# Modulation rows, first norm and five input panels by quarters instead of halves, at the start of a two-block kernel

## What is computed

```python
c_act = jax.nn.silu(c)
mod = c_act @ w_ada[l] + b_ada[l]                 # 2048 -> 6 * 2048
sh1, sc1, g1, sh2, sc2, g2 = [m[:, None, :] for m in jnp.split(mod, N_MOD, axis=-1)]
h = rms_norm(x, norm_mix_g[l]) * (1.0 + sc1) + sh1
proj = h @ w_in[l]                                # 2048 -> 8192
u, q, k, v, ga, gb = jnp.split(proj, split_at, axis=-1)
y_ssm = s5_branch(u, ...)                         # scan over tokens, 64 groups of 64 states
y_att = moba_attention(q, k, v, rel_bias)
merged = sigmoid(ga) * (y_ssm @ w_proj_ssm) + sigmoid(gb) * (y_att @ w_proj_attn)
x = x + g1 * (merged @ w_out[l])
```

## Time and profile before

| | us |
|---|---|
| runs: median (range) | 3000.81 (3000.13 to 3002.28) |
| profiled execution, its own time | 3000.71 |
| its span | 2999.4 |
| busy PE, DVE, ACT, POOL in the span | 2931.9, 2023.6, 1379.4, 239.4 |
| chain that ended last | PE 86%, DVE 7%, DMA 3%, issue 2% |

### The profile page before, as it was taken

The page is one execution under the profiler, slowest core; times in us unless marked ns, Lnnn a source line. Parts: engine busy times, 40 slices in busy tenths (PEclk is TensorE's granted clock), DMA queues, the critical chain, the costliest instruction groups (busy, mean ns, idle before and its releaser), DMA issues.

```text
span 2999.4 us, 42350 instructions
## 1 busy us (share of the span) xinstructions
PE 2931.9 (98%) x17149; PEld 2513.0 (84%) x17149; DVE 2023.6 (67%) x2359; ACT 1379.4 (46%) x1686; POOL 239.4 (8%) x256
## 2 busy tenths in 40 slices
PE   6999999999999999999999999999999999999998
PEld 3778899788888888888989987778898888888886
DVE  5489878997767655556887776674557545555555
ACT  3343344444444444345565655554445444444443
POOL 6835410000000000000000000000000000000000
PEclk9999999999999999999999999999999999999999
DMA  9967688896777766665556565456555666666664
GB/s 350 329 213 210 209 295 297 302 319 203 236 257 257 235 187 193 194 186 172 174 171 196 174 192 155 155 161 195 186 176 175 190 189 188 192 190 192 192 191 149
DMA packets 303520, 631.67 MB, mean 211 GB/s; under 512 B 21872, under 2 KB 26384, under 8 KB 302752
## 3 DMA queue, kind: packets, MB, share of 16 engines
q1 hardware_dynamic: 298496, 618.74, 64.9%
q10 hardware_dynamic: 2800, 5.33, 0.5%
q0 software_dynamic: 2032, 4.90, 0.5%
HBM read 624.68 MB, written 4.21 MB: 210 GB/s over the span
## 4 chain that ended last, share of the span: by engine, by line
PE 86%; DVE 7%; DMA 3%; issue 2%; ACT 1%; ACTq 0%; DVEq 0%
PE PS L1026 16%; PE PS L1042 15%; PE PS L1044 15%; PE PS L1043 15%; PE PS L1030 8%; PE PS L1013 5%; PE PS L1015 5%; PE PS L1014 5%; DVE wlo L1991 2%; DMA raw<-in_w_ada 1%; DVE aacc L1980 1%; ACT whi L2519 1%; PE PS L691 1%; DMA raw<-in_w_in 1%; PE PS L824 1%
## 5 line engine op out<-in xcount | busy, mean ns | idle before, releaser
L1991 DVE TENSOR_TENSOR wlo<-raw,whi 128x1024 fp32r<-128x1024 f32 x857 | 1070.4, 1254 | 729.6 <-ACT whi L2519 729.1
L2519 ACT ACTIVATE whi<-raw 128x1024 fp32r<-128x1024 f32 x857 | 904.5, 1059 | 1077.2 <-PE PS L1044 570.1
L1042 PE MATMUL PS<-whi,R 128*128 128x512 f32 x2144 | 847.2, 395 | 7.3 <-DVE R L1496 5.4
L1043 PE MATMUL PS<-whi,R 128*128 128x512 f32 x2144 | 836.0, 390 | 0.0
L1044 PE MATMUL PS<-wlo,R 128*128 128x512 f32 x2144 | 835.9, 390 | 0.0
L1026 PE MATMUL PS<-R,whi 128*128 128x512 f32 x2048 | 516.5, 394 | 10.8 <-DVE R L1903 5.4
L1042 PEld LDWEIGHTS PS<-whi,R 128*128 128x128 f32 x2144 | 403.0, 188 | 102.1 <-issue 7.6
L1044 PEld LDWEIGHTS PS<-wlo,R 128*128 128x128 f32 x2144 | 402.9, 188 | 85.6
L1043 PEld LDWEIGHTS PS<-whi,R 128*128 128x128 f32 x2144 | 403.2, 188 | 81.5 <-issue 1.0
L1013 PE MATMUL PS<-R,whi 128*128 128x256 f32 x1536 | 439.8, 286 | 7.5 <-DVE wlo L1991 6.0
L1026 PEld LDWEIGHTS PS<-R,whi 128*128 128x128 f32 x2048 | 371.3, 190 | 78.4 <-issue 11.5
(11 more groups left out here) (424 smaller groups left out, 1728.8 us busy)
## 6 DMA issues: line engine op xcount, KB each, us to landing
raw<-in_w_in SPq DMA_DIRECT2D x275, 512.0 KB, 4.3
raw<-in_w_ff SPq DMA_DIRECT2D x175, 512.0 KB, 4.4
raw<-in_w_ada SPq DMA_DIRECT2D x136, 512.0 KB, 5.2
raw<-in_w_mlp_up SPq DMA_DIRECT2D x128, 512.0 KB, 3.8
raw<-in_w_mlp_down SPq DMA_DIRECT2D x128, 512.0 KB, 4.4
...
```

Source lines behind the costliest of these rows:

```text
L1042: pe.matmul(o, hi, whi[:, s, w], start=first, stop=False)
L1043: pe.matmul(o, lo, whi[:, s, w], start=False, stop=False)
L1991: v.tensor_tensor(wlo[:, i % SPN, :], words(j), whi[:, i % SPN, :].bitcast(F32), ALU.subtract).then_inc(lo_done, 1)
L2519: a.activation(whi[:, i % SPN, :], words(j), ACT.Copy).then_inc(hi_done, 1)
```

## The change

- The row units hold 512 columns of sc1's and the same 512 of sh1's part. 16 of them give a quarter: four tiles of h. The row is copied, closed and normed four times, after row units 15, 31, 47 and 63, each time in the tick's own `side`, and ScalarE's copy stands ahead of that tick's weight splitting.
- 27 weight ticks instead of 17 lie between the row ticks, the first after row unit 18 (before: 33), and 30 units are prepared there.
- The five part panels are computed by quarters: 15 panels of two units. ScalarE copies the first quarter's, VectorE adds the second's and third's (`part_more`, 10 new instructions of 128 by 1024); the last quarter is what `both_halves` adds.
- x's transposes, its deviation and the first norm's factor come sooner (ticks 3, 7, 10 instead of 6, 13, 28 after the start), the factor is copied to SBUF; the four matrices' ticks lie between 28 and 62; the branch's input matrix is loaded by ScalarE at row tick 13 instead of at the start.
- x is saved to DRAM in four pieces instead of one. SSM0 is 32 instead of 24. v0 comes ahead of q0 and k0, two of the gb panels are read out one tick later, and the eight attention heads start 5 to 14 and 2 to 11 ticks after k0 and k1 instead of 2 to 11 after v0 and v1.

```diff
-NTAKEN = 17
+QUARTER = 16
+NTAKEN = 27
 NEARLY = NTAKEN + 3
-TAKEN = {33: 0} | {36 + n * 27 // (NTAKEN - 1): n + 1 for n in range(NTAKEN - 1)}
-EARLY = {31: (0,)} | {a - 3: (n,) for a, n in TAKEN.items() if n} | {61 + n: (NTAKEN + n,) for n in range(3)}
+TAKEN = {18 + n * 45 // 26: n for n in range(NTAKEN)}
+EARLY = {a - 3: (n,) for a, n in TAKEN.items()} | {61 + n: (NTAKEN + n,) for n in range(3)}
 NWIDE = 56
 NXN = 16
-SSM0 = 24
+SSM0 = 32
...
-    for i in range(5):
-        panel("part", i, w_in, 0, 8, i * 512 if i < 2 else 4096 + (i - 2) * 512, h, by_h, a_once.at("part%d" % i), i > 1)
+    by_h = lambda k: (h_ready, k + 1)
+    by_quarter = lambda q: lambda k: (h_ready, 4 * q + k + 1)
+    halved = [i * 512 if i < 2 else 4096 + (i - 2) * 512 for i in range(5)]
+
+    for q in range(3):
+        for i, c0 in enumerate(halved):
+            panel("part", 5 * q + i, w_in, 4 * q, 4, c0, h_from[q], by_quarter(q),
+                  (part_added, 5 * q + i - 4) if q else a_once.at("part%d" % i), i > 1)
     for i in range(2):
-        panel("u", i, w_in, 8, 8, i * 512, h_b, by_h_b, (evac_v["u"], i + 1))
+        panel("u", i, w_in, 12, 4, halved[i], h_from[3], by_quarter(3), (evac_v["u"], i + 1))
     for i in range(3):
-        panel("ga", i, w_in, 8, 8, 4096 + i * 512, h_b, by_h_b, v_once.at("ga%d" % i), True)
+        panel("ga", i, w_in, 12, 4, halved[2 + i], h_from[3], by_quarter(3), v_once.at("ga%d" % i), True)
     panel("ga", 3, w_in, 0, 16, 4096 + 1536, h, by_h, (evac_a["ga"], 4), True)
     for i in range(4):
         panel("gb", i, w_in, 0, 16, 6144 + i * 512, h, by_h, (evac_a["gb"], i + 1), True)
     for i in range(2):
-        for name, c0 in (("q", 1024), ("k", 2048), ("v", 3072)):
+        for name, c0 in (("q", 1024), ("k", 2048), ("v", 3072)) if i else (("v", 3072), ("q", 1024), ("k", 2048)):
...
+    def row_src(q, kt):
+        return wada[kt * P:(kt + 1) * P, 0:2 * D].rearrange("p (g d) -> p g d", g=2)[:, :, 512 * q:512 * q + 512]
+
     def weight_unit(n):
         return "w", n, 4 if panel_of[n].nk == 4 else 2, unit_src[n]
 
     for a in range(NADA):
-        units.append(("row", a, 1, ada_src(a % 2, a // 32, a % 32 // 2)))
+        units.append(("row", a, 2, row_src(a // QUARTER, a % QUARTER)))
...
-    row_bank, row_close_bank = (0, 7), (2, 5)
-    rstd1 = PS[:, 4, T:2 * T]
+    row_bank, row_close_bank = (0, 7, 4, 7), 6
+    rstd1 = rstd[:, :]
 
     def norm_tile(k):
-        return PS[:, ((2, 3, 5) if k < 8 else (5, 6, 7))[k % 8 % 3], 0:T]
+        return PS[:, 5 + k % 2, 0:T]
...
-    X_TURN, COLUMNS, STD1, FACTOR1 = -NADA + 6, -NADA + 10, -NADA + 13, -NADA + 28
-    B_TURN, MATRICES_C = -NADA + 11, len(TAKEN) + 2
-    MATRIX = (-NADA + 17, -NADA + 18, -NADA + 19, -NADA + 37)
-    MATRIX_TURN = (-NADA + 23, -NADA + 26, -NADA + 30, -NADA + 40)
-    ROW_CLOSE, NORM1 = [-33, len(TAKEN)], [-32, len(TAKEN) + 1]
+    X_TURN, STD1, COLUMNS, FACTOR1, BIAS, B_TURN = (-NADA + t for t in (3, 7, 8, 10, 11, 22))
+    B_LOAD, X_SAVE = -NADA + 13, [NTAKEN + t for t in (-1, 2, 5, 8)]
+    ANGLES, PARAMETERS, MATRICES_C = -NADA + 17, -NADA + 18, len(TAKEN) + 2
+    MATRIX = (-NADA + 28, -NADA + 40, -NADA + 47, -NADA + 57)
+    MATRIX_TURN = (-NADA + 34, -NADA + 45, -NADA + 53, -NADA + 62)
+    ROW_COPY = [-NADA + 15 + QUARTER * q for q in range(4)]
+    ROW_CLOSE = [-NADA + 15, -NADA + 32, -NADA + 48, len(TAKEN) - 1]
...
-            free[4] = h_ready, 8
+            free[4] = a_once.at("factor1")
 
         def row_matmuls(n, j):
-            q, g, kt = n // 32, n % 2, n % 32 // 2
+            q, kt = n // QUARTER, n % QUARTER
             pe.wait_ge(*landed(j))
             if n == 0:
                 pe.wait_ge(*v_once.at("cact"))
-            if n == 32:
-                wait_bank(row_bank[1])
+            elif kt == 0:
+                wait_bank(row_bank[q])
+                free[row_bank[q]] = row_copied, q + 1
             for part in range(4):
                 o = 32 * part
-                t = pe.matmul(PS[o:o + 1, row_bank[q], g * T:g * T + T], cact[:, kt:kt + 1], words(j)[:, part * T:part * T + T],
-                              start=(n % 32 == 0), stop=(kt == 15), skip_group_check=True)
+                t = pe.matmul(PS[o:o + 1, row_bank[q], 0:T], cact[:, kt:kt + 1], words(j)[:, part * T:part * T + T],
+                              start=(kt == 0), stop=(kt == QUARTER - 1), skip_group_check=True)
             t.then_inc(row_done, 1)
 
         def row_close(q):
-            bank = row_close_bank[q]
             pe.wait_ge(row_copied, q + 1)
-            if q:
-                wait_bank(bank)
-            for g in range(2):
-                for c in range(2):
-                    o = 512 * q + T * g + P * c
-                    t = pe.matmul(PS[:, bank, 8 * g + 4 * c:8 * g + 4 * c + 4], aacc[:, o:o + P], ident[:, 0:P:32],
-                                  start=(g + c == 0), stop=True, skip_group_check=True)
+            wait_bank(row_close_bank)
+            for c in range(2):
+                o = T * q + P * c
+                t = pe.matmul(PS[:, row_close_bank, 4 * c:4 * c + 4], aacc[:, o:o + P], ident[:, 0:P:32],
+                              start=(c == 0), stop=True, skip_group_check=True)
             t.then_inc(row_turned, 1)
-            if q:
-
-                for bank in (4, 5, 6, 7):
-                    free[bank] = (h_ready, 16)
-            yield
+            free[5] = free[6] = h_ready, 4 * q + 4
...
-            s8 = slice(8 * q, 8 * q + 8)
+            s4 = slice(4 * q, 4 * q + 4)
             tile = norm_tile
             v.wait_ge(modrow, q + 1)
-            if q == 0:
-                v.wait_ge(m_copied, 6)
-            v.scalar_tensor_tensor(A1[:, s8], mod[:, 16 + 8 * q:24 + 8 * q], 1.0, cols[:, C_G1 + 8 * q:C_G1 + 8 * q + 8],
+            if turned_in(q):
+                v.wait_ge(m_copied, turned_in(q))
+            v.scalar_tensor_tensor(A1[:, s4], mod[:, 16 + 4 * q:20 + 4 * q], 1.0, cols[:, C_G1 + 4 * q:C_G1 + 4 * q + 4],
                                    ALU.add, ALU.mult).then_inc(v_own, 1)
             v.wait_ge(v_own, vt.one())
-            v.wait_ge(*p_once.at("stat1"))
-            v.wait_ge(*a_once.at("b"))
-            for n in range(10):
+            v.wait_ge(*a_once.at("factor1"))
+            for n in range(6):
                 if n > 1:
-                    k = 8 * q + n - 2
+                    k = 4 * q + n - 2
                     v.wait_ge(n1_hi, k + 1)
                     v.scalar_tensor_tensor(h.lo(k), tile(k), mod[:, k:k + 1], h.hi(k).bitcast(F32),
                                            ALU.add, ALU.subtract).then_inc(h_ready, 1)
-                if n < 8:
-                    k = 8 * q + n
-                    if n > 2:
-                        v.wait_ge(h_ready, k - 2)
+                if n < 4:
+                    k = 4 * q + n
+                    if n > 1:
+                        v.wait_ge(h_ready, k - 1)
                     v.scalar_tensor_tensor(tile(k), X3[:, k, :], A1[:, k:k + 1], rstd1, ALU.mult, ALU.mult).then_inc(n1_scaled, 1)
-                if n == 9:
-                    yield
...
+        def part_more(x):
+            i, q = x.i % 5, x.i // 5
+            v.wait_ge(*passed("part", x.i))
+            v.wait_ge(*(a_once.at("part%d" % i) if q == 1 else (part_added, i + 1)))
+            v.tensor_tensor(half_sum(i), banks(x), half_sum(i), ALU.add).then_inc(part_added, 1)
+            yield
+
         def both_halves(x):
             i = x.i
             v.wait_ge(*passed(x.name, i))
             if x.name == "u":
-                v.wait_ge(*a_once.at("part%d" % i))
+                v.wait_ge(part_added, 6 + i)
                 v.tensor_tensor(fv(U + 1024 * i, 1024), banks(x), half_sum(i), ALU.add).then_inc(evac_v["u"], 1)
             else:
                 if i == 0:
                     v.wait_ge(h_ready, 16)
-                    v.wait_ge(x_saved, 16)
-                v.wait_ge(*a_once.at("part%d" % (2 + i)))
+                v.wait_ge(x_saved[i], 16)
+                v.wait_ge(part_added, 8 + i)
...
+        def x_save(p):
             a.wait_ge(x_copied, 8)
-            a.dma_start(scr_x, fv(XT, 4096)).then_inc(x_saved, 16)
+            a.dma_start(scr_x[:, 1024 * p:1024 * p + 1024], fv(XT + 1024 * p, 1024)).then_inc(x_saved[p], 16)
...
-            a.wait_ge(row_done, 32 * q + 32)
-            a.copy(aacc[:, 512 * q:512 * q + 512], PS[:, row_bank[q], :]).then_inc(row_copied, 1)
+            a.wait_ge(row_done, QUARTER * (q + 1))
+            a.copy(aacc[:, T * q:T * q + T], PS[:, row_bank[q], 0:T]).then_inc(row_copied, 1)
...
+            if n in ROW_COPY:
+                row_copy(ROW_COPY.index(n))
...
```

More of the change, by code:

```diff
@@ L106, with __init__, at @@
 class Operand:
-    def __init__(self, R, *blocks):
-        self.R, self.blocks = R, blocks
+    def __init__(self, R, *blocks, first=0):
+        self.R, self.blocks, self.first = R, blocks, first
+    def at(self, k):
+        k += self.first
```

(44 more changed lines are left out.)

88 lines of the change are left out of this document (42 added, 46 removed).

## The result

| us | before | changed |
|---|---|---|
| median of 6 runs | 3000.96 (2999.41 to 3004.08) | 3015.64 (3010.79 to 3018.83) |
| profiled execution, its own time | 3000.71 | 3015.87 |
| its span | 2999.4 | 3014.6 |
| PE busy, idle in the span | 2931.9, 67.5 | 2936.9, 77.7 |

The ratio of the times is 1.0048, with a 95% interval of 1.0039 to 1.0058: the changed kernel is slower by 0.5%, where 2993.5 and faster was forecast, and 3004 was the end of the range. Of the 15.2 us between the spans 10.2 are idle time of PE and 5.0 are busy time: the same 17149 matmuls, more of them at the low clock.

What follows compares the result with a forecast made beforehand. TensorE's matmuls were taken to bound the kernel, with loads bounding the row phase: 12.9 us gained, less 4.6 of moved branch work and 1.1 behind the rows, is 7.2 off 3000.7, so 2993.5; range 2985 to 3004.

Steps and rivals of the forecast that it cites:

- The first panel: Start of unit 0, now waiting for a quarter of the rows: forecast at 44.3 us, before 64.61.
- the row 389 against 407: GB/s of weight loads in 2 KB runs against row loads alone; 389 taken for the new row loads, +1.25 us.
- the other estimate: Skill-based reading for halved row-load runs: 2% of loading time, some 1.0 us at row 63 rather than 2.2.
- The sum of the phase: PE work from unit 0 to the end of unit 26: 115.1 us, ending at 159.4, 12.9 us ahead.
- The glu wait: PE's 5.4 us wait at a glu panel later on; its going was only a bound, -5.4, costed at 0.
- The new adds: Seven VectorE adds behind the rows instead of two, at 1.22 us each, +6.1; at most 2.32 each.
- The closes: Three further norms during the rows: waits hidden by units, costed at nothing, bounds 0 and 2.8 us each.
- The loads on the way: Loads up to row 63: 52.4 MB at 352 GB/s land near 153, PE there at about 156, hidden by 3 us.
- The norm-chain rival: The norm stalls PE at each further close: 1.61 + 1.21 three times, 8.4 us, giving 3001.9; chance 0.08.
- The rest: Work moved among engines after 205.7, such as x saves, v0 first and later heads: costed at 0, bounds -5.4 and +3.
- One low stretch: Unit 0 running at the low clock: 1.7 us taken, bounds 0 and 2.9.
- The VectorE behind the rows: Weight ticks 26 to 42: VectorE 7.7 us longer than PE, 4.3 spare, PE waits 3.4, net loss 1.1 us.

Runs made afterwards that it cites:

- e5: Changed kernel with only the list of VectorE's counted points put in program order, no instruction moved: 3008.96 us, ratio 1.0027 to the kernel before.
- e7: Changed kernel with list in order, norm over two ticks, matrices off the closes and acc sums from unit 36: 2995.35 us, ratio 0.998 to before.
- e6: Changed kernel with the list in program order and the norm's tiles over two ticks: 3001.5 us, ratio 1.0003 to the kernel before.
- e11: e7 with the matrices back at the changed kernel's ticks 28, 40, 47, 57: 2998.53 us, ratio 0.9997 to the kernel before.
- e8: e7 with 24 instead of 27 weight units between the row units and without the list's edit: 3004.66 us, ratio 1.0011 to the kernel before.
- e4: Changed kernel with acc sums begun at weight unit 36 instead of at once at unit 30: 3009.5 us, ratio 1.0032 to the kernel before.

## Why the prediction was wrong

**Right.** The first panel started 0.65 us from the forecast (runs with the same start lie between 43.9 and 45.5, so no closer could be told), and the 2 KB runs were slower by 4%, as the row 389 against 407 said and not by the 2% of the other estimate. The 2.2 us given for this at row 63 is too low by its own figures: 64 loads of 0.524 MB at 389 instead of 407 are 3.8; the sum does not use it. The sum of the phase was sound where nothing waited: the second unit and its row take 3.06 + 0.98 (49.91 to 53.95, two row units), where 2.92 + 0.69 + 0.42 was priced, and a unit with one row unit 3.06 + 0.54 = 3.6. The glu wait shrank, which was left as a bound. The new adds took 1.22, the price of L1507: two inputs with one in PSUM are not held up beside GpSimd.

**The step that failed first: "The closes", costed at nothing.** Measured, two of the three closes cost 6.40 us of waits (its bounds were 0 and 2.8 each, the third took 4.30) and, by the starts behind them, about 3 more of low clock. The prediction said that the next quarter's panels begin several units after their close. They do not: the close stands just ahead of unit 9, 18 or 27, and unit 10, 20 or 30 opens the next quarter. One, two and three units are between; at the second close one unit of 3 us is to cover 5.5 us of norm and the split behind it, at the third two are. And it looked at PE's wait for h alone. What is queued behind the norm was not followed on to what waits for it. A matrix's turn needs a PSUM bank that the norm's tiles hold: 2.10 at the second close. The next unit needs its split: 4.30 at the third. Both are waits of PE straight for VectorE. And SyncE needs the raw buffer that the split gives back. "The loads on the way" had 3 us of cover and was worked out from what the DMA engines can move, 352 GB/s, not from when they are asked: at two closes SyncE stands still for 4.1 (87.54 to 91.68) and 11.2 us. One wait for a row load followed, 2.31. The norm-chain rival had this place and was nearest: it priced 8.4 us at three closes, where 6.40 at two were measured. It took them from PE's waits at the first close, when only row units were loaded, whose buffers TensorE gives back; there was no split in the queue.

**The term that was not in the sum: the wrong count.** 6.7 us by e5. Nothing in the trace of before could show it. It could be read from the changed program: a list of points and VectorE's order, side by side. I had held the reordering to be free ("The rest").

**The clock.** One low stretch, 1.7 us, was in the sum, and unit 0 bore it: 4.42 (44.95 to 49.37), where 2.92 + 1.7 was priced. In the changed kernel between unit 1 and 250 the clock falls after five waits: behind the 4.30, matmuls of unit 20 start 0.21 us apart instead of 0.12 for 3.4 us, and the unit takes 4.53 (136.50 to 141.03) instead of 3.06. So a wait of 4.3 cost 5.8. Over the span the matmuls took 5.0 us longer, net of low stretches that only the kernel before has.

**The VectorE behind the rows** was sized at 3.4 us of wait. Once the list was in order, 2.0 was seen in e5 and 1.5 in e7 as waits for VectorE: that term was close. One price in it was low: acc sums are 1.62 us each in the earlier trace rows, and three more are 4.9, not 4.0. And e5 still has a wait of 2.32 at 191.14 for ScalarE's copy of an output matrix, which was in no term; it is 0.33 or less in e7.

The balance, by medians: 3015.64, list -6.7, norm over two ticks -7.5, acc sums later -3.0 (e6 to e11), matrices off the closes -3.2 (e11 to e7), 2995.35. Each kernel's ratio is known to about 0.1%, 3 us, so the first two steps are shown and the last two are so only in their sum. The forecast 2993.5 is 1.9 away from that, but four edits stand between, and in e7 unit 27 starts 5 us later than was forecast, so the closeness is partly luck: the change could give about what was forecast, but not as it stood.

Open: why e8 lost, how much of the closes' price came through SyncE, why unit 27 starts no sooner than 162.8 in any run, and which part of e4's gain is of the acc sums and which of the spread. The heads' ticks and the place of panel v0 hang together with SSM0 and were not tried alone.
